# Last z products and a short convolution behind the first scores, seven ring slots free at first, second group's output products in quarters

## The reference, cut to what matters

```
h   = rmsnorm(x);  z = h @ W_in                      # 1024 x 2432 = 19 blocks of 128 columns
A = conformer convolution(z)   B = RWKV-7(z)
C = gate_b * conv3(gate_c * h_c)   D = causal pooling(z)
x1  = x + concat(A, B, C, D) @ W_out                 # 1024 x 1024
q   = rmsnorm(x1) @ Wq;  scores against 2 x 128 keys, per 8 heads
top 16 of the 256 sums of two top-16 lists  -> 16 experts e per position and head
x2  = x1 + sum_s softmax_s * gelu(<u[e_s], rmsnorm(x1)>) * v[e_s]
out = rmsnorm(x2)
```

## Time and profile before

| | us |
|---|---|
| median of 3 runs (1665.66 to 1673.72) | 1668.51 |
| the profiled execution, its own time | 1671.36 |
| its span | 1669.6 |
| busy: PE / DVE / POOL / ACT | 1220.8 / 1236.3 / 916.7 / 709.3 |
| gathers: first issue, count | 257.49, 520 |
| DMA moved, mean | 605.42 MB, 363 GB/s |
| granted TensorE clock, mean | 0.842 |

### The profile page before, as it was taken

One profiled execution on the slowest core, in us unless ns is written; L12 is line 12 of the kernel. 1 busy time (PEld: TensorE's weight loads), 2 busy tenths in 40 slices (PEclk: granted clock), 3 DMA queues, 4 the chain that ended last, 5 costly groups with the idle time before them and its releaser, 6 DMA issues.

```text
span 1669.6 us, 19415 instructions
## 1 busy us (share of the span) xinstructions
PE 1220.8 (73%) x5360; PEld 615.6 (37%) x5360; DVE 1236.3 (74%) x2935; ACT 709.3 (42%) x2021; POOL 916.7 (55%) x1135
## 2 busy tenths in 40 slices
PE   8998898766676877677886767675766676767564
PEld 6887756322233544332332323232322232323110
DVE  3878767788878887677778777777667776767775
ACT  3322223555454444344455654443444443434444
POOL 0364012557565766454566655565665576656662
PEclk9999999888797998788998778787878877767777
DMA  7321468999999999999999999999999999999996
GB/s 217 115 89 51 98 217 290 420 417 378 417 419 396 415 417 396 416 415 416 353 418 419 417 419 417 418 418 418 410 406 418 412 409 414 417 404 407 420 412 280
DMA packets 109308, 605.42 MB, mean 363 GB/s; under 512 B 22905, under 2 KB 25337, under 8 KB 42641
## 3 DMA queue, kind: packets, MB, share of 16 engines
q0 software_dynamic: 74880, 545.29, 79.8%
q1 hardware_dynamic: 34304, 58.89, 10.8%
q10 hardware_dynamic: 16, 0.02, 0.0%
HBM read 600.97 MB, written 3.19 MB: 362 GB/s over the span
## 4 chain that ended last, share of the span: by engine, by line
DMA 37%; PE 27%; DVE 16%; POOL 6%; issue 6%; ACT 4%; DVEq 3%; POOLq 0%; SPq 0%
DMA arena<-in_uv,arena 35%; PE ps L1011 11%; DVE arena L1979 8%; PE ps L612 5%; POOL arena L2233 4%; DVEq L1414 3%; PE ps L962 3%; DVE arena L1417 3%; POOL arena L2232 2%; PE ps L684 2%; DVE arena L1423 2%; PE ps L981 1%; ACT arena L1344 1%; PE ps L663 1%; ACT arena L1340 1%
## 5 line engine op out<-in xcount | busy, mean ns | idle before, releaser
L1011 PE MATMUL ps<-arena 128*64 128x512 f32 x2048 | 659.5, 779 | 368.5 <-ACT arena L1344 367.2
L1979 DVE CUSTOM_DVE_ANT_0 arena<-arena 128x1024 f32<-128x1024 f32 x520 | 640.8, 1234 | 292.6 <-DMA arena<-in_uv,arena 270.7
L2233 POOL DMA_INDIRECT arena<-in_uv,arena x520 | 617.8, 1188 | 87.2 <-POOL arena L2232 17.3
L2232 POOL TENSOR_TENSOR arena<-arena 1x1 f32<-1x1 f32 x520 | 216.7, 417 | 501.0 <-PE ps L1011 412.2
L1011 PEld LDWEIGHTS ps<-arena 128*64 128x64 f32 x2048 | 151.0, 164 | 754.3 <-ACT arena L1344 521.1
L1338 ACT ACTIVATE arena<-arena 128x1 f32<-128x1 f32 x520 | 105.1, 202 | 699.4 <-DVE arena L1979 697.1
L1344 ACT ACTIVATE arena<-arena 128x64 f32<-128x64 f32 (+1 forms) x520 | 181.4, 349 | 16.9
L1340 ACT ACTIVATE arena<-arena 128x1 f32<-128x1 f32 x520 | 153.2, 295 | 16.9
L1417 DVE TENSOR_TENSOR arena<-arena 128x512 f32<-128x512 f32 (+9 forms) x312 | 134.6, 432 | 21.6 <-ACT arena L1096 7.4
L612 PE MATMUL ps<-arena 128*128 128x264 f32 (+1 forms) x608 | 141.2, 386 | 0.3 <-DVE arena L1417 0.3
L962 PEld LDWEIGHTS ps<-arena 128*128 128x128 f32 x1024 | 126.9, 205 | 38.4 <-issue 37.3
(11 more groups left out here) (177 smaller groups left out, 937.8 us busy)
## 6 DMA issues: line engine op xcount, KB each, us to landing
arena<-in_win SPq DMA_DIRECT2D x38, 512.0 KB, 3.4
arena<-in_wqk SPq DMA_DIRECT2D x60, 256.0 KB
arena<-in_wout SPq DMA_DIRECT2D x24, 512.0 KB, 4.9
arena<-in_uv,arena POOLq DMA_INDIRECT x520
arena<-in_xp SPq DMA_DIRECT2D x4, 512.0 KB, 6.6
out_yp<-arena SPq DMA_DIRECT2D x4, 512.0 KB
arena<-in_wqk SPq DMA_DIRECT2D x15, 128.0 KB
arena<-in_const SPq DMA_DIRECT2D x1, 864.0 KB, 7.7
```

Source lines behind the costliest of these rows:

```text
L1011: last = mm(ps[64 * q:64 * q + 64, b + c, :], diag[:, (s + q) % 8, :], ring[:, SLOT_OF[TOPK * u + s + q], D + 512 * c:D + 512 * c + 512], ...
L1979: v.tensor_tensor_reduce(out=here, in0=here, in1=row, scale=1.0, scalar=0.0, op0=MUL, op1=ADD, accum_out=hsel[:, u % 2, s:s + 1]).then_inc ...
L2232: pool.tensor_tensor(carrier[:, 1:2], carrier[:, 0:1], carrier[:, 0:1], ALU.add).then_inc(S["carried"], 1)
L2233: pool.indirect_dma_start(out=ring[:, SLOT_OF[k], :], out_offset=None, in_=a["uv"][:, :], in_offset=bass.IndirectOffsetOnAxis(ap=idx[:, t, ...
```

## The change

- **Ring.** `wring` moves below `hT[1]`, which now fills slot 7. Seven slots (k = 0 to 6) are first uses, slot 7 comes at k = 14. Gather 5 waits for the fifth W_out block of tile 1, gather 14 (`FRESH`) for the last copy of z.
- **Last z products.** The order `BLOCKS` is 31 z blocks, then the 13 blocks of W_out, with no z block between. The seven last z products (numbers 31 to 37) read two buffers of their own (`zlate`): two loads after tile 1's weights, then one more each time a product is done. On PE number 31 stands behind tile 1's output products, number 32 before the second query, and 33 to 37 one behind each of the first five `sums`.
- **Short convolution** of group 1 goes from POOL to DVE (`short_second`), between group 0's mixer and `residual(0)`.
- **Conformer of group 1**: three taps fewer in the last chunk, the last six behind `second_features(0, 1)`; mean, variance, centring, scaling, root, sigmoid and product each some steps later. DVE's choice for unit 1 is split: steps 0 to 5 ahead of dot 4, 6 to 11 behind it.
- **Group 1's mixer** on DVE begins only when all z are copied.
- **Output products of tiles 2 and 3** are made in four parts of 4 matmuls, due at ticks 0, 2, 4 and 5 of a tile in place of two of 8 at 0 and 4.

```diff
-SLOT_OF = [0, 1, 2, 3, 4, 0, 1, 2, 3] + [(5, 6, 7, 4, 0, 1, 2, 3)[k % 8] for k in range(8 * 65)]
-FREE = (0, 1, 2, 3, 4, 9, 10, 11)
-FRESH = 9
+SLOT_OF = 2 * list(range(7)) + [(7, 0, 1, 2, 3, 4, 5, 6)[k % 8] for k in range(8 * 65)]
+FREE = (0, 1, 2, 3, 4, 5, 6, 14)
+FRESH = 14
...
+            def late_weights(i):
+                if i >= 2:
+                    sp_.wait_ge(S["z_done"], ZFRONT + i - 1)
+                sp_.dma_start(zlate[i % 2].rearrange("p a b -> p (a b)"), a["win"][ZORDER[ZFRONT + i][0]]).then_inc(d_late[i % 2], 16)
+
             sp_.wait_ge(S["tails_done"], 3)
+            for i in range(2):
+                late_weights(i)
...
+            for i in range(2, len(ZORDER) - ZFRONT):
+                late_weights(i)
...
             query(0)
+            score(0)
+            first_out(1, 1, 2)
+            conf_mean(1)
+            first_out(1, 2, 8)
+            zcol()
             conf_variance(1)
-            score(0)
-            first_out(1, 1, 8)
-            zcol(3)
             turned(1, 0)
             turned(1, 1)
+            zcol()
             query(1)
             score(1)
             pe.wait_ge(S["z_copied"], Z_HIGH)
-            sums(0, 0)
-            zcol()
-            sums(0, 2)
-            zcol()
+            for s in range(0, 10, 2):
+                sums(0, s)
+                zcol()
...
-                for s in range(5 if u == 0 else 0, slots):
+                for s in range(4 if u == 0 else 0, slots):
                     k = TOPK * u + s
                     weigh(u, s)
-                    if k == 5:
+                    if k in (5, 7, 9):
+                        zc()
+                    if k == 7:
                         conf_sigmoid(1)
...
+            def short_second():
+
+                sw = col("sw", 0, 2 * SK).rearrange("p (a b) -> p a b", b=SK)
+                dve.wait_ge(S["short_done"], 1)
+                dve.wait_ge(S["z_copied"], ZCOUNT[(18, 1)])
+                dst = yb[:, 4:6, 0:GT]
+                lk(tt(qpad[:, :, SK - 1 + GT:], zc8[:, :, GA:NT], zh8[:, :, GA:NT], MUL))
+                for k in range(SK):
+                    for cc in range(2):
+                        o, i, w = dst[:, cc], qpad[:, cc, GT + k:GT + k + GT], sw[:, cc, k:k + 1]
+                        last = stt(o, i, w, o, MUL, ADD) if k else ts(o, i, w, MUL)
+                    lk(last)
+                tt(dst, dst, zb8[:, :, GA:NT], MUL).then_inc(S["short_done"], 1)
...
                     if k == 4:
-                        for step in range(STEPS - 1):
+                        for step in range(6, STEPS - 1):
                             choose(1, step)
+                    elif k == 6:
+                        conf_scale(1)
                     elif k == 7:
                         choose(1, STEPS - 1)
...
+                    elif k == 5:
+                        pool.wait_ge(S["block_used"], KT - 1 + 5)
```

More of the change, by code:

```diff
@@ L138 @@
 ZFRONT = 31
-Z_HIGH = 35
+Z_HIGH = 33
 def z_bank(j):
@@ L297, in build @@
         o_h = o_r + 3344 + 256
-        o_hb = o_ring + RING * ROW - 3 * KT * 128 - KT * GT
-        o_w = o_hb + KT * GT
-        assert o_w + 3 * KT * 128 == o_up and o_h + KT * GA <= o_hb and o_hb >= o_ring + 5 * ROW
+        o_hb = o_ring + RING * ROW - KT * GT
+        o_w = o_hb - 3 * KT * 128
+        assert o_h + KT * GA <= o_w and o_hb == o_ring + 7 * ROW and o_w >= o_ring + 5 * ROW
         hT = (at(o_h, KT, GA), at(o_hb, KT, GT))
@@ L350, in build @@
         assert 11 * NT + len(ASIDE) * D <= o_elb + 4 * 2 * GT - o_p
+        zlate = [at(o, KT, 128) for o in (o_p + 8792, o_p + 10184)]
+        assert 11 * NT + len(ASIDE) * D <= 8792 and 10184 == 19 * NT + 304 and 10184 + D <= 12288 - D
         ctmp = at(o_r + 2816, 2, NS, CK)
@@ L434, in build @@
         d_w = [sem(f"d_w{i}") for i in range(3)]
+        d_late = [sem(f"d_late{i}") for i in range(2)]
         d_row = [sem(f"d_row{i}") for i in range(RING)]
@@ L603, in zcol @@
                     i, g = ZORDER[j]
-                    n = BLOCK_OF[("z", j)]
                     lo, hi = BANDS[g]
-                    pe.wait_ge(d_w[n % 3], 16 * (n // 3 + 1))
+                    if j < ZFRONT:
+                        n = BLOCK_OF[("z", j)]
+                        pe.wait_ge(d_w[n % 3], 16 * (n // 3 + 1))
+                        w = wring[:, n % 3]
+                    else:
+                        pe.wait_ge(d_late[(j - ZFRONT) % 2], 16 * ((j - ZFRONT) // 2 + 1))
+                        w = zlate[(j - ZFRONT) % 2]
                     if j >= 2:
@@ L611, in zcol @@
                     for k in range(KT):
-                        last = mm(ps[:, z_bank(j), 0:hi - lo], wring[:, n % 3, k, :], hT[g][:, k, :], start=(k == 0), stop=(k == KT - 1))
+                        last = mm(ps[:, z_bank(j), 0:hi - lo], w[:, k, :], hT[g][:, k, :], start=(k == 0), stop=(k == KT - 1))
                     last.then_inc(S["z_done"], 1)
@@ L658, in first_out, with project_out @@
                     last.then_inc(S["block_used" if j < KT - 1 else "out_mm"], 1)
[L660 to L664, removed]
+            def project_out(t, nh, part):
+                y = Y_ROWS[t][1]
+                for j in range(4 * part, 4 * part + 4):
+                    last = mm(ps[:, 5 + nh, :], y[:, OUT_ORDER[j], :], w_blocks[j][:, 512 * nh:512 * nh + 512], start=(j == 0), stop=(j == KT - 1))
+                if nh and part:
                     last.then_inc(S["out_mm"], 1)
@@ L845, in mixer, with project @@
                 tiles = (2, 3, TILES)
-                def project(k, nh):
+                def project(k, nh, part):
                     t = tiles[k]
-                    if not nh:
+                    if not nh and not part:
                         pe.wait_ge(S["rwkv_out"], 2)
@@ L854, in project @@
                     if t < TILES:
-                        project_out(t, nh)
-                    else:
+                        project_out(t, nh, part)
+                    elif part:
                         project_samples(nh)
                 for k in range(3):
[L860 to L863, removed]
+                    for piece in range(4):
+                        yield C_OUT + 7 * k + (0, 2, 4, 5)[piece]
+                        project(k, piece // 2, piece % 2)
                 for k in range(3):
@@ L1053, in unit @@
                     return
-                for s in range(4 if u == 0 else 0, TOPK, 2):
+                for s in range(10 if u == 0 else 0, TOPK, 2):
                     sums(u, s)
@@ L1327, in _ @@
             queries(0)
-            conf_root(1)
             act.wait_ge(d_const, 16)
@@ L1817, in _ @@
                 first.until(C_CH + 6 * c + 3)
-                taps(3)
+                taps(3 if c < GC - 1 else 0)
             first.until(C_LN + 2)
-            taps(64)
+            taps(3)
             first.finish()
+            short_second()
             residual(0)
@@ L1826, in _ @@
             second_features(0, 1)
-            conf_center(1)
+            taps(64)
             def choose(u, step):
@@ L2032, in _ @@
             dot(0, 3)
+            for step in range(6):
+                choose(1, step)
             for u in range(NU + 1):
@@ L2197, in _ @@
             windows_second()
-            short(1)
+            pool.wait_ge(S["short_done"], 2)
             pool.tensor_copy(tails[:, :, 45:47], qpad[:, :, SEQ:SEQ + 2]).then_inc(S["tails_done"], 1)
```

36 lines of the change are left out of this document (14 added, 22 removed).

## The result

| | before | after |
|---|---|---|
| median of the runs, us | 1668.53 | 1699.14 (1695.06 to 1705.28) |
| ratio, 95% interval | | 1.0177 [1.0151, 1.0202] |
| the profiled execution, own time, us | 1671.36 | 1698.31 |
| its span, us | 1669.6 | 1696.5 |
| granted TensorE clock, mean | 0.842 | 0.840 |

The change makes the kernel slower by 1.77%, or 29.5 us of 1668.5; the two medians lie 30.6 us apart, and what follows goes by the ratio. The forecast was 1684.0 with a range of 1673 to 1698: the direction holds, the size does not, and the measured time lies 1.1 us above the range.

The account below looks back on a forecast made before the run. From about 290 us a stream of gathers at 418 GB/s was taken to bound the kernel. Stream 20.5 us later less 5 for quarters: 15.5 more, 1671.36 to 1686.9 profiled, 2.9 above the median, so 1684.0; range 1673 to 1698.

Parts of the forecast that it names:

- the sum: Whole kernel: stream 20.5 us later at gather 17, less 5 for output products in quarters, gives 15.5 us more.
- Front: Kernel start up to the first gather: residual at 225.0, convolution hidden by 0.5 us, first gather at 250.3, 7.2 us earlier.
- Sums 0 at 271.1, sums 4 at 286.4: PE after the first gathers: sums 0 at 271.1, before at 278.66; sums 4 at 286.4, 1.0 behind DVE's dot.
- Loads: SyncE after z 35: z block 37 and query weights, 1.6 MB, take 8 us (6.9 alone, 9.4 behind one gather).
- Half clock: PE's three pauses before sums 4, query 2 and sums 8 cost 5 us at half clock (bounds 0 and 5.3).
- Softmax 312.2, sums 8 316.9, z 37 322.4: Chain behind z 36: ACT's softmax, DVE's dots, sums 8, z 37; gather 14 at 323.0, or 328 with half clock.
- Gather 17 then has landed at 341: Gather 17 lands at 341, after gather 14 at 328; before, dot 17 ran at 320.49; stream 20.5 us later.
- rival 3: After gather 14: DVE's crowded work makes gather 32's unit 2 indices 5 to 10 us late; 1689 to 1696, chance 0.09.
- Quarters: Output products of tiles 2 and 3: backlog peaks near 6, not 10, gaining 5 us (bounds 0 and 6.7).
- The range: Whole kernel: 1673 to 1698, holding the forecast's bounds (1675.5 to 1694.5) and rival 3, without Rival 1.
- Rival 1: At gather 14: z 37 copied by about 298, so the stream never stops; 14 us less, 1654.5, chance 0.09.
- At 312.5 or earlier the kernel is no slower: Sign deciding Rival 1: if gather 14 is issued at 312.5 or earlier, the kernel is no slower.

Follow-up runs that it names:

- a: Changed kernel with the second head's query weights loaded right behind z block 34, ahead of blocks 35 to 37: 1694.61 us, ratio 1.0136.
- g: Changed kernel with z products 33 to 37 made earlier, all ahead of sums 6 and query 2, ACT's copies at slots 4, 5, 7: 1675.22 us, ratio 1.0023.
- d: Kernel before the change with only its output products of tiles 2 and 3 cut in quarters: 1668.74 us, ratio 0.9983.
- g to j: g; g with query weights ahead of z block 37; g with softmax 1 before last copies; that plus slot 7 at gather 21: 1.0023, 1.0023, 1.0007, 0.9991.
- c: Changed kernel with slot 7 first used by gather 21, so the gate on the last z copy moves from gather 14: 1699.87 us, ratio 1.0174.
- b: Changed kernel with ACT making sigmoid and unit 1's softmax ahead of the copy of z product 36: 1691.81 us, ratio 1.0123.
- e: Changed kernel with both the moves of a and b, query weights early and softmax 1 ahead of the copy: 1689.29 us, ratio 1.0093.
- f: Changed kernel with the moves of e, and slot 7 first used by gather 21 as in c: 1687.94 us, ratio 1.0092.

## Why the prediction was right in kind and wrong in size

The profiled execution grew by 26.95 us where the sum had 15.5. The gap of 11.45 has three terms: 6.1 at gather 14, 4.0 from there to dot 17, 1.4 at the quarters. Between the medians it is 3.7 more, since the profiled execution of the kernel before lay 2.8 above its median and that of the changed kernel 0.8 below its own. The measured time is only 1.1 us above the range, so without any one of these four it would lie inside; the gap to the forecast is their sum.

- **Front** ("7.2 us earlier"): 6.4. W_out, paced by its loads, ended 1.3 later than counted (residual at 228.76 - 2.43 = 226.3, forecast 225.0); the convolution is hidden, as said.
- **Sums 0 at 271.1, sums 4 at 286.4**: 271.92 and 287.66, within 1.3. This has the 2.4 us in it by which the execution ran late from the start: counted from the first W_out block, both came 1.2 to 1.6 us earlier than forecast.
- **Loads ("I take 8")**: the failed step. z product 35 ended at 294.91 and query 2 began at 307.53, 12.6 us, 4.6 more than assumed, and above the upper end of 9.4. That end counted one gather beside the loads, but gathers 11, 12 and 13 went out at 291.06, 293.44 and 299.33. With 2.5 us for each, 6.9 + 7.5 = 14.4 would have been the end to take. That the three gathers made the loads late is argued from these rows and from the 403 GB/s of the window 296 to 306; no run takes the gathers away. a and g show the wait itself to be removable, by other orders.
- **Half clock ("I take 5")**: the number is right and the kind of loss too, the terms are not. Sums 4 took 2.95, z 35 4.37, query 2 6.12 against my 4.5, sums 8 3.64: in order 1.0 + 0.7 + 1.6 + 1.7 = 5.1 over the figures of the sum. The prediction speaks of three pauses, but its 5.3 comes out only as 2 x 1.65 for sums 4 and 8 and 2 x 1 for z 35 and 37. Of that 3.5 came, z 37 taking 3.73 with no loss; the 1.6 of the query, not in it, made up the difference, which is luck. The granted clock was 0.60 and 0.53 in the windows 300 to 310 and 320 to 330, and in g, with no such pause, 7.20 for two z products and 3.84 for the query. The Trainium skill (TensorE: Matmul & The Clock Gate, "What's actually happening") has a throttled clock as the default that activity releases; the trace agrees, and the forecast with the 5 us was nearer than without. Not every pause costs: behind one of 2.08 us sums 6 took 1.94, full clock.
- **Softmax 312.2, sums 8 316.9, z 37 322.4**: each came 9.0, 9.0 and 10.8 later (321.2, 325.9, 333.2), and the links between them have the lengths that were counted. So gather 14 at 334.07 is the forecast 328 plus 6.1: 1.3 of a later start, 4.6 of loads, the rest small.
- **"Gather 17 then has landed at 341"**: this assumed that data ends dot 17's wait, 13 us behind gather 14. It took 17.0, the second term that was too small, since DVE waited for score 2 (the 4.00 above), itself behind sums at 3.68 and a score at 1.23 in place of 0.71. A second stop behind the first is what rival 3 names, with a chance of 0.09, but not by this mechanism: it had DVE too busy and gather 32 waiting for the indices of unit 2. Here DVE stood idle, waiting for the score, and gather 32 is 29.0 us late, less than gather 17. The stop comes on top of the forecast, not in its place.
- **Quarters ("I take 5")**: alone they give 2.8 (d), with an interval that still holds the 5. In the pair of traces the lateness fell from 30.6 at dot 17 to 26.95 at the end, 3.6 in all, of which some 2.4 at the quarters by the medians above. The argument that a backlog of 6 us makes no hole failed: PE's pairs came about as predicted (sums at 833.75, 842.83 and 848.33, so 9.1 and 5.5 apart) and the two windows around them still show

```profile
840.00:850.00 10.00, 10.00 (x31) 3.35 (x29) 6.67 (x12) 2.78 (x8) 3.90 (x4) 1.00 0.93 359
850.00:860.00 10.00, 8.15 (x30) 2.85 (x28) 7.90 (x20) 9.59 (x24) 7.33 (x10) 1.00 0.94 334
```

- **The range** failed at its upper end: 1.5 us for slower loads where 4.6 came, and none for a second stop, which was kept apart as a case of its own although both can hold at once.
- **Rival 1** (the gate is covered) is refuted for the changed kernel: gather 14 at 334.07, where it needed 298. In g to j, with gather 14 at 303 to 311, even a nearly covered gate did not give its 14 us, as the slots stood full. "At 312.5 or earlier the kernel is no slower" missed narrowly: g, at 303.39, is slower by 0.2%, with an interval that excludes no change.
- **What the text blamed.** It said that gather 14's wait for the last z copy decides. Experiment c shows that the loss does not need this gate: the same lateness comes through DVE, which waits for softmax 1 behind the same z products. The cause is the place of z products 35 to 37, as g shows for some 26 of the 29.5 us; what the ring slot that they guard adds was not told apart.

## What to carry to other kernels

When a buffer's release is moved later, look at what the consumers do at that time: if the same late chain also holds the consumer, the releaser named by the producer's wait is only one of two gates, and what helps is to shorten the chain. A step that is put behind a pair of sums inherits every wait of that pair (data, softmax, query, and the loads that the step itself lets go), so count the chain through all engines before moving fill work from ahead of a query to behind it. More free slots at the start brought nothing that lasted here, while the engines that empty them were busy with something else.

## What the runs showed of the hardware

- 1.6 MB of plain loads on one queue, issued in 2.5 us (294.94 to 297.4) while gathers were in flight, were ready for use 12.6 us after the first issue; DMA moved 403 GB/s from 296 to 306. One load of 0.5 MB took 4.4 us.
- What work costs behind a pause of PE is not told by that pause. Sums 4 stood behind the same idle of 4.60 or 4.61 us and the same order of work in the changed kernel and in a, b, c, e and f, and took 2.95, 3.68, 2.94, 3.36, 2.98 and 3.68 us, where 1.94 is full clock.
- Nor do two pauses close together settle it. In a, e and f z product 35 stood behind a second idle of 2.32, 3.04 and 2.52 us: it took 6.31 and 6.16 in a and e, and 3.73, full clock, in f. The sums 6 behind it took 3.43 and 3.58 in a and e and 1.94 in f, behind the same 2.07 or 2.08 us. What made f different no run here shows.
